# A chunk scan's small products with 128 stationary columns, and its head sums through the whole array

## The reference

```python
kk = kk / jnp.maximum(jnp.sqrt(jnp.sum(kk * kk, axis=-1, keepdims=True)), 1e-12)   # per head
def step(s, inp):
    r_t, w_t, k_t, v_t, aa_t, bb_t = inp
    sa = jnp.einsum('bhij,bhj->bhi', s, aa_t)
    s = s * w_t[:, :, None, :] + sa[..., None] * bb_t[:, :, None, :] + v_t[..., None] * k_t[:, :, None, :]
    return s, jnp.einsum('bhij,bhj->bhi', s, r_t)
...
mean = jnp.mean(y, axis=-1, keepdims=True)                     # per head
var = jnp.mean(jnp.square(y - mean), axis=-1, keepdims=True)   # per head
bonus = (jnp.sum(r_h * k_h * r_k.astype(f32), axis=-1, keepdims=True) * v_h).reshape(bsz, t, c)
```

## Time and profile before

| | |
|---|---|
| time, median of 3 runs | 3130.36 us (3126.57 to 3135.87) |
| profiled execution: its time, its span | 3138.41 us, 3136.5 us |
| TensorE busy (matmul), share of the span | 2991.5 us, 95%, 29234 instructions |
| TensorE weight loads | 2886.6 us, 92% |
| VectorE, ScalarE, GpSimd busy | 1799.3 us (57%), 1022.9 us (33%), 953.7 us (30%) |
| the chunk scan in the trace | about 1657 to 2133 us |

### The profile page before, as it was taken

One profiled execution on the slowest core, in us unless ns is written; L12 is line 12 of the kernel. 1 busy time (PEld: TensorE's weight loads), 2 busy tenths in 40 slices (PEclk: granted clock), 3 DMA queues, 4 the chain that ended last, 5 costly groups with the idle time before them and its releaser, 6 DMA issues.

```text
span 3136.5 us, 66763 instructions
## 1 busy us (share of the span) xinstructions
PE 2991.5 (95%) x29234; PEld 2886.6 (92%) x29234; DVE 1799.3 (57%) x1884; ACT 1022.9 (33%) x1281; POOL 953.7 (30%) x549
## 2 busy tenths in 40 slices
PE   8999999999999997889998989998999999999998
PEld 7899999999999997889996777787999999999997
DVE  7766765555656567512206767773566555565657
ACT  6433411111111113633326767774311111111113
POOL 2222223222222223313314555552132322222221
PEclk9999999999999999999999999999999999999999
DMA  3111111111111111142232222213111111111111
GB/s 108 46 44 41 41 42 41 48 48 41 48 41 48 41 48 34 72 183 84 91 111 82 73 60 72 78 43 102 42 48 41 41 48 48 41 48 41 48 41 71
DMA packets 88684, 185.66 MB, mean 59 GB/s; under 512 B 29024, under 2 KB 53088, under 8 KB 88416
## 3 DMA queue, kind: packets, MB, share of 16 engines
q1 hardware_dynamic: 81504, 154.73, 15.5%
q10 hardware_dynamic: 6912, 26.84, 2.1%
HBM read 145.01 MB, written 36.53 MB: 58 GB/s over the span
## 4 chain that ended last, share of the span: by engine, by line
PE 80%; DVE 13%; ACT 4%; issue 2%; POOL 1%; DMA 0%; DVEq 0%; SPq 0%; ACTq 0%; POOLq 0%
PE PS L1306 65%; PE PS L1516 12%; DVE T L1817 3%; DVE X L1817 2%; PE PS L1442 2%; DVE T L1832 2%; ACT T L512 1%; ACT L512 1%; DVE HL L1827 1%; DVE T L1827 1%; PE PS L1396 1%; PE PS L1358 1%; DVE G L1817 1%; ACT UV L512 1%; DVE T L1822 1%
## 5 line engine op out<-in xcount | busy, mean ns | idle before, releaser
L1089 POOL TENSOR_TENSOR WL<-RAW,WH 128x1024 fp32r<-128x1024 f32 x204 | 495.4, 2428 | 1393.1 <-ACT WH L512 1389.4
L1306 PE MATMUL PS<-HH,WH 128*128 128x364 f32 x3456 | 771.8, 331 | 31.4 <-DVE HL L1827 12.5
L1306 PE MATMUL PS<-HH,WL 128*128 128x364 f32 x3456 | 768.5, 331 | 0.0
L1306 PE MATMUL PS<-HL,WH 128*128 128x364 f32 x3456 | 765.2, 330 | 0.0
L1306 PEld LDWEIGHTS PS<-HH,WH 128*128 128x128 f32 x3456 | 601.5, 189 | 39.2 <-issue 15.3
L1306 PEld LDWEIGHTS PS<-HH,WL 128*128 128x128 f32 x3456 | 606.7, 189 | 0.0
L1306 PEld LDWEIGHTS PS<-HL,WH 128*128 128x128 f32 x3456 | 603.8, 189 | 0.0
L512 ACT ACTIVATE WH<-RAW 128x1024 fp32r<-128x1024 f32 x204 | 216.6, 1062 | 823.3 <-PE PS L1306 806.6
L1817 DVE TENSOR_TENSOR T<-PS,T 128x1092 f32<-128x1092 f32 x110 | 142.5, 1296 | 551.9 <-PE PS L1306 535.1
L1817 DVE TENSOR_TENSOR X<-PS,X 128x1092 f32<-128x1092 f32 (+2 forms) x240 | 292.8, 1220 | 232.9 <-PE PS L1306 214.1
L1306 PE MATMUL PS<-PH,WH 128*128 128x364 f32 x1248 | 278.1, 331 | 10.2 <-DVE X L1817 5.2
(11 more groups left out here) (191 smaller groups left out, 3428.0 us busy)
## 6 DMA issues: line engine op xcount, KB each, us to landing
RAW<-weights SPq DMA_DIRECT2D x204, 512.0 KB, 3.3
scratch<-T ACTq DMA_DIRECT2D x31, 546.0 KB, 3.1
scratch<-SR ACTq DMA_DIRECT2D x14, 546.0 KB, 2.9
X<-xT SPq DMA_DIRECT2D x8, 546.0 KB, 7.6
T<-scratch_m SPq DMA_DIRECT2D x8, 512.0 KB, 3.3
KK<-scratch SPq DMA_DIRECT2D x16, 192.0 KB, 2.6
LW<-scratch SPq DMA_DIRECT2D x16, 192.0 KB, 2.6
AA<-scratch SPq DMA_DIRECT2D x16, 192.0 KB, 3.2
```

The costliest lines, as they stand in the source:

```text
L1089: pool.tensor_tensor(out, full, hi, ALU.subtract).then_inc(*t.made(event))
L1306: mm = pe.matmul(acc[:, j, :], a, b[:, j * CW:(j + 1) * CW], start=(i == 0 and q == 0), stop=(i == len(blocks) - 1 and q == 2))
```

## The change

`products` issues one matmul per head and chunk instead of two: the two neighbouring slots `h` and `h + 1` of `BK` are its 128 stationary columns, and its output is all 128 partitions of bank `3 + h`. `sums` (and the first key squares) issue one matmul with all 128 rows and columns of the block `C_BD`. The products and their operands are the same numbers. The counts that the readers wait for follow: `k_g` rises by two for each group instead of four, `s_kk`, `s_bon`, `s_mean` and `s_var` by one instead of two. No other step, and no step's place in the order, changes.

```diff
--- before.py
+++ after.py
@@ -446,7 +446,7 @@
 
                 if job + 4 < JOBS:
                     f, b = divmod(job + 4, NB)
-                    sp.wait_ge(*t.at("k_g", 8 * (job + 2)))
+                    sp.wait_ge(*t.at("k_g", 4 * (job + 2)))
                     sp.wait_ge(*t.at("k_bonus", job + 2))
                     for tile, j in ((LW, 0), (KK, 4), (AA, 1), (RR, 3), (VV, 5)):
                         load(b, f, tile, j, f"dma_in{b}")
@@ -983,7 +983,7 @@
                 def group_ln():
 
                     if has_n:
-                        act.wait_ge(*t.next("s_var", 2))
+                        act.wait_ge(*t.next("s_var"))
                         run(q1, PS[:, 2, 0:(nz - na) * CHUNK], ACT.Ln, "k_gln", scale=1.0 / CHUNK, bias=GN_EPS, own=False)
 
                 def group_exp():
@@ -1474,9 +1474,8 @@
 
                 pe.wait_ge(*t.at("taken0", M_OUT // 2))
                 pe.wait_ge(*t.at("k_sq", 1))
-                for h in range(HEADS):
-                    pe.matmul(PS[HALF[h], 2, 0:BW], CO[HALF[h], C_BD + h * CHUNK:C_BD + (h + 1) * CHUNK], X2[HALF[h], 0:BW],
-                              start=True, stop=True, skip_group_check=True).then_inc(*t.made("s_kk"))
+                pe.matmul(PS[:, 2, 0:BW], CO[:, C_BD:C_BD + P], X2[:, 0:BW],
+                          start=True, stop=True, skip_group_check=True).then_inc(*t.made("s_kk"))
 
             for j in range(3):
                 for f in range(j == 0, KT):
@@ -1526,9 +1525,7 @@
                     if bank2:
                         pe.wait_ge(*t.at(*bank2))
                     bank2 = (reader, count)
-                    for h in range(HEADS):
-                        mul(PS[HALF[h], 2, 0:src.shape[-1]], CO[HALF[h], C_BD + h * CHUNK:C_BD + (h + 1) * CHUNK],
-                            src[HALF[h]], event)
+                    mul(PS[:, 2, 0:src.shape[-1]], CO[:, C_BD:C_BD + P], src, event)
 
                 def key_squares():
 
@@ -1690,10 +1687,9 @@
                     else:
                         held(("k_gm", 2 * q + 1))
                     for i in range(ga, gz):
-                        for s in range(2):
-                            for h in range(HEADS):
-                                mul(tile(3 + h, (h + s) % 2, i - ga, P), BK[HALF[h], i, s if h == 0 else 2 - s, :],
-                                    AR[HALF[h], i, :, :].rearrange("p s c -> p (s c)"), "k_g" if i == gz - 1 else None)
+                        for h in range(HEADS):
+                            mul(PS[:, 3 + h, (i - ga) * P:(i - ga + 1) * P], BK[HALF[h], i, h:h + 2, :].rearrange("p s c -> p (s c)"),
+                                AR[HALF[h], i, :, :].rearrange("p s c -> p (s c)"), "k_g" if i == gz - 1 else None)
 
                 def value_turn():
 
@@ -2199,7 +2195,7 @@
                 def floor():
 
                     if has_k:
-                        dve.wait_ge(*t.next("s_kk", 2))
+                        dve.wait_ge(*t.next("s_kk"))
                         ts(X2[:, klo:khi], PS[:, 2, 0:khi - klo], 1e-24, None, ALU.max, ALU.bypass, "k_max", own=False)
 
                 def scan():
@@ -2238,7 +2234,7 @@
                 def bonus():
 
                     if has_p:
-                        dve.wait_ge(*t.next("s_bon", 2))
+                        dve.wait_ge(*t.next("s_bon"))
                         if q == 0:
                             dve.wait_ge(*t.at("dma_spill0", SPILLS[0]))
                         if has_n:
@@ -2249,7 +2245,7 @@
 
                     if has_p:
                         ga, gz = groups(pb, 4)[g]
-                        dve.wait_ge(*t.next("k_g", 4))
+                        dve.wait_ge(*t.next("k_g", 2))
                         n = gz - ga
                         tt(G[:, ga:gz, :, 0:P].rearrange("p n h c -> p h n c"),
                            PS[:, 3:5, 0:n * P].rearrange("p h (n c) -> p h n c", c=P),
@@ -2284,7 +2280,7 @@
                 def centred():
 
                     if has_n:
-                        dve.wait_ge(*t.next("s_mean", 2))
+                        dve.wait_ge(*t.next("s_mean"))
                         stt(flat(Y)[:, ncols], PS[:, 2, 0:(nz - na) * CHUNK], -1.0 / CHUNK, flat(Y)[:, ncols],
                             ALU.mult, ALU.add, "k_cent", own=False)
```

## The result

Over 15 runs of each kernel the median went from 3135.77 to 3141.33 us, ratio 1.0021 with a 95% interval of 1.0012 to 1.0029: +0.21%, some 6.6 us. The change is slower, by less than the 0.3% that I set as the bound of "the same". I forecast +0.93%, 29 us: the sign was right and the size wrong by a factor of four, and the reason for that is what the runs were for. That the measured median lies in the range of 3138 to 3180 us is luck: the range was built on 3130.4 us, the median of three runs of before, and before's median over 15 runs is 5.4 us higher.

A forecast was written before the change was run, and what follows sets the result against it. TensorE's stream was taken to bound the chunk scan. Means 7.7, variances 0, key squares 15.8, products and bonus 9.9, first key squares −0.3 and fewer records −4 gave +29 us: median 3130.4 to 3159.4 us, range 3138 to 3180.

The forecast's parts named there:

- What bounds the kernel: Chunk scan: TensorE is most of the chain of waits, so time added to its stream mostly lengthens the scan.
- Change of tile shape: TensorE between tile shapes: each change into the full array costs 0.195 us, into other shapes 0.14 us.
- Products, array time: Chunk products: half the matmuls go, but array time stays the same, as pairs of 64x128 tiles run together; 0 us.
- that rival: Chunk products: pairs of 64x128 tiles take turns instead of running together, +30 us, giving 3188 us; chance 0.06.
- Key squares, products and bonus: Key squares lose overlap with `left(3)`, 15.8 us; shape changes around products and bonus sum, partly covered, 9.9 us.
- Variances, waits, DMA: Variances' shape changes hidden by 0.6 us of cover, 0; fewer completion counts and unmoved DMA, 0.
- Means: Means sum before `powers`: 0.335 us a job on the path for shape changes, 7.7 us over 23 steady jobs.
- The work terms: Scan costs without the gaps: means 7.7, variances 0, key squares 15.8, products and bonus 9.9, first key squares −0.3 us.
- Fewer records: TensorE's 20.6 us of unexplained gaps shrink with a 5.2% shorter instruction stream: −4 us, bounds 0 and −20.6.
- The sum: Whole kernel: all terms add to +29 us, median 3159.4 us, +0.93%.
- The instruction stream was the limit: TensorE's scan: all 20.6 us of gaps go, only lost overlap of 8.7 us stays; 3118.5 us, faster; chance 0.06.
- The added time is covered: Scan: added TensorE time mostly hides behind VectorE and ScalarE, some 7 us left; 3133 us; chance 0.10.

The follow-up runs named there:

- experiment 4: The whole change with the key squares put back in two quarters of the array: ratio 0.9986 to the kernel before.
- experiments 7 and 10: One kernel on two chips: products with 128 stationary columns and variances through the full array, on the kernel before; ratios 0.9995 and 0.9976.
- experiment 6: The kernel before with every sum's columns issued in two halves, 760 records more for the same array time: ratio 1.0012 (0.9998 to 1.0026).

## Why the prediction was wrong

*What bounds the kernel:* right. The scan's chain became 93.8% TensorE, and time added where nothing else waited did lengthen it.

*Change of tile shape:* right for the drain, 0.09 us at each change, 0.15 us from start to start. Right for the full array's first load (0.43 us between its passes, 0.323 + 0.105). Wrong for the 64x128 tile: I read 0.05 us off `key_turn`'s transposes, and the f32 products show 0.10 (their second pair is 0.207 us after the first, the others 0.112). By the Trainium skill's "TensorE: Matmul & The Clock Gate", section on LDWEIGHTS, it is 0.107 (an estimate, 128 columns over its 1.2 GHz), which I had set aside for the row: here the trace agrees with the page, and `key_turn` was the wrong neighbour.

*Products, array time:* right. No time gained, pairs run together; that rival is out.

*Key squares, products and bonus:* right in kind, a little too large. I took 0.75 + 0.45 = 1.20 us a job. From the sum to the 128-row tile it is +0.78 (1.57 for 0.79), and the lost overlap is confirmed by experiment 4. Up to `products(0)`, whose start had some slack before (1.89 us behind the 128-row tile, and 1.71 with the sums alone changed), +0.71 is left in two kinds of job and +0.53 in the third (shortest stretches, as above), and from `products(0)` to `key_turn` it is +0.12 to +0.45, 0.28 on the mean. That is 0.93 us together. The cover of 0.30 us that I took for three changes of shape is what the two jobs above show, 0.475 − 0.18.

*Variances, waits, DMA:* the variances cost nothing, as experiments 7 and 10 show: with them alone in the full array the key squares start no later. With all the sums changed they start 0.3 us later in one kind of job, some 3 us in the scan, which I did not have and cannot assign.

*Means:* predicted 0.335 a job, found 0.10 to 0.27, 0.16 on the mean. The sum's second pass and the drain out of it are there (0.84 for 0.65), but part is taken back before `solved`, which now follows `powers` after 0.53 us instead of 0.61.

*The work terms* together were 33 us and came to about 26.

*Fewer records:* this is the step that failed, and it was a term mis-sized: −4 us taken, −17.3 us measured as gaps and −27.7 us as stops of the loads. I scaled the gaps by the share of removed instructions. Stops at the end of each block of 256 do not scale so. They are what a fetch lacks in a block that is used up too soon, and a stream 12% slower per block (3.93 to 4.39 us) takes that away almost everywhere.

*The sum* is then +26 − 28 us, nothing, which is what the scan shows in the trace, beside +6.6 us (3.8 to 9.1) in the medians. Both errors made the forecast too high, the work terms by some 7 us and the gaps by some 24. Those 31 us are more than the 22 by which the forecast missed; the 6.6 us of the medians themselves are not placed by the traces.

*Signs.* I had named as signs of being wrong the gaps "much below 15" and a scan of 476 us in place of 505: both came. The waits for ScalarE and VectorE shrank too, from 20.7 to 14.4 us in TensorE's rows. The signs named for being right (starts 0.15 us apart, `left(3)` after the second pass, pairs at 0.11 us) came as well, since the costs were nearly right and only what paid for them was missed.

*Rivals.* "The instruction stream was the limit" (0.06) was half right: the gaps did nearly all go, but changes of shape still cost, because they fall mostly where no gap was. My argument against it was poor: 33 gaps for 28,152 records is few only until one counts by blocks of 256, of which the scan has some 110. "The added time is covered" (0.10) was right for the products alone and for 0.30 us around the bonus sum, wrong for the rest.

*Open.* A block's own length does not decide alone: of the 13 blocks after the change that were used up in under 3.6 us none ended in a stop, of the 46 before 30 did. Why single fetches start late is not settled; the 1.7 us gap at 1803.9 us stood beside heavy data loads, others of 0.6 us beside none. With the products alone the stops fell by 21.4 us and the scan by 13.2. The fetch was never changed by itself, only the stream over it, and experiment 6 shows no effect of the number of instructions alone.

## What to carry to other kernels

Before costing an edit, find one repeated unit of work that has no unexplained idle time in it, or put one together from the shortest stretches of several, and compare units, not means: here the mean job moved by 0.01 us and the job without gaps by about 1.24. Ask of each idle time that nothing ends whether it stands a constant number of instructions behind the last one; if so, the stream is short of code, longer work is partly free and shorter work partly wasted. A product that fills the whole array must be priced with what ran in the other quarters (0.78 us for a saving of two matmuls here), and slack behind another engine is spent once, by whichever edit comes first.

## What the runs showed of the hardware

- TensorE's code comes in pieces of 256 instructions, one packet of 16 KB each (231 packets for 59,245 instructions before, 225 for 57,773 after), and in 1,307 blocks none was begun sooner than 2.08 us after its packet's start. Of the blocks used up in under 3.3 us about half end in a stop (77 of 149 in the twelve scans, 19 of 22 before), of those over 3.9 us one in thirty (26 of 797). At 1771 to 1775 us the packet was the only transfer, and there was a gap even so.
- Two f32 matmuls of 64 rows and 128 columns in the two halves of the array start together and follow each other at 0.112 us, as four quarter tiles do.
- The load of an f32 64x128 tile whose shape is new is exposed for 0.10 us, as that of the full array (0.105); for the transposes in tiles of that shape it was 0.05.
- Leaving a shape for another takes 0.09 us more from start to start than staying (about 0.15 for 0.058 in the small tiles, 0.21 for 0.112 in 64x128, 0.41 for 0.323 in the full array).
